# A convolution stage with three places for raw weights, three product buffers and later side transfers

## The chip, the cores and the metric

The kernel runs on one core of a Trainium2 chip. The metric is the device time of one execution in microseconds (us); the median over several executions is compared. One execution is also recorded by the hardware profiler, and all rows below are from that one.

## The reference, cut to what matters

A decoder trunk of two layers over 512 tokens with 1024 features. The change touches the first layer only, a convolution layer:

```python
def conformer_conv_branch(h, w_in, b_in, conv_w, conv_b, norm_g, norm_b, w_out, b_out):
    proj = h @ w_in + b_in                      # 512 x 1024 @ 1024 x 6144
    val, glu_gate, z = jnp.split(proj, 3, axis=-1)
    u = val * jax.nn.sigmoid(glu_gate)          # 2048 channels
    u = lax.conv_general_dilated(               # causal, 31 taps, one filter a channel
        u, conv_w[:, None, :], window_strides=(1,), padding=[(CONV_KERNEL - 1, 0)],
        dimension_numbers=('NWC', 'WIO', 'NWC'), feature_group_count=CONV_WIDTH) + conv_b
    u = jax.nn.silu(layer_norm(u, norm_g, norm_b))
    u = u * jax.nn.silu(z)
    return u @ w_out + b_out
```

Then comes `h = layer_norm(alpha * h + y, g, b)`, and an attention layer that the change does not touch. All is float32; a matrix product is made of three products of rounded parts (a high part and a low part of each operand, without low times low).

## The kernel before, in words

**Chunks.** The input projection of the first layer is cut into 48 chunks of 128 output channels, numbered c = 0 to 47. Chunks 2t and 2t + 1 (t = 0 to 15) are value and gate of channel tile t; chunks 32 + i (`Z0` + i) are z of tile i. Chunk c takes these steps, each engine in the order of its program:

- SP issues the load of 512 KB into a raw place `w_raw[c % 2]` (`load_columns`, L605), once chunk c - 2 has been split (`raw_free`), since there are two places.
- ACT rounds it into `w_hi[c % 4]` (`split_hi`, L1082), after the load has landed.
- POOL subtracts: `w_lo = w_raw - w_hi` (`split_lo`, L861).
- PE makes 24 matmuls (8 steps of 128 features, three products each, `columns`, L1961) into one of three PSUM banks.
- ACT keeps the bank (`keep_value` L1088, `keep_gate_half` L1094, `keep_z` L1228), POOL multiplies value and gate into `u` (`glu`, L873).

**Convolution beside it.** It is spread over all engines while PE makes the chunks:

- DVE makes twelve of the sixteen tiles (`convolve`, L1556), one tap an instruction, in two chains for each tile. ACT starts most chains (`start_chains`, L1136 and L1139). When DVE is done with its tiles it sums them (L1540, L1542) with a sum that POOL has made of others (`pool_csum`, L968), and PE multiplies the sum by ones for the mean, in the middle of chunk 43 (`sum_over_channels`, L2077). From there DVE, ACT and POOL make the variance.
- Tiles 1 and 7 (`GROUPED_TILES`): ACT multiplies four taps at a time (`BEFORE_GATING`), and POOL issues a DMA that adds the 1 MB to sums (`add_group`, L902). Before it issues one, POOL waits for the one before to have landed. The last taps of these tiles, and the first 22 of tile 4 (`LATE_TILE`), are single products: ACT writes one into `tap_product` (four buffers, `tap_times_u` L1176), and POOL adds it to `acc` one step later (`add_products`, L923). `AFTER_GATING`, `BEFORE_GATING[10]` and `IN_Z` say in which step which taps are made.
- Tiles 8 and 12 (`MATRIX_TILES`, m = 0 and 1) are made on PE as four packs each (`pack`, L2048 to L2051), after chunks 26 to 29 and 35 to 38. SP writes the tile's input to DRAM (`keep_u`, L611 and L613), reads it back shifted as stacks (`stack_u`, four DMAs for a pack, L622); ACT keeps each pack in one of two buffers (`keep_pack_after`, L1105), since all packs use one bank; SP moves its four parts (`move_parts`, L636) to free tiles.

**Order.** There is no planner: each engine's program is written out in one order. SP's order around the change is: the load of chunk c, then what `stack_after(c)` gives to that place, then the load of c + 1. ACT's order in step t (`value_gate`) is: w_hi of 2t, w_hi of 2t + 1, value of t - 1, packs kept, grouped taps, chain starts, gate of t - 1, products. POOL's is: w_lo of 2t and of 2t + 1, products of step t - 1 added, glu of t - 1, the group's DMA, and in steps 10 and 14 the low part of a matrix tile's input (L940), in step 15 the two matrices of the second matrix tile (L934).

Of the kernel before, what the change touches and what calls it, by code (L numbers as in the profile page):

```python
# [32 lines left out]
P = 128  # L33
# [53 lines left out]
RAW_SLOTS = 2  # L87
SLOTS = 4
# [34 lines left out]
def trunk_kernel(nc, x, positions, ln_g, ln_b, a_w_in, a_b_in, a_conv_w, a_conv_b, a_norm_g,  # L123
# [14 lines left out]
    with ExitStack() as ctx:  # L138
# [99 lines left out]
        tap_product = [at(f"tap_product{i}", reg_e, (2 + i) % 4 * TILE, [P, SEQ]) for i in range(4)]  # L238
# [84 lines left out]
        small_landed, table_landed = sem("small_landed"), sem("table_landed")  # L323
        w_landed = [sem(f"w_landed{i}") for i in range(RAW_SLOTS)]
# [203 lines left out]
        def landed_value(c):  # L528

            extra = 16 if isinstance(c, int) and c >= ROPE_CHUNK and (c - ROPE_CHUNK) % RAW_SLOTS == 0 else 0  # L530
            return 16 * (c // RAW_SLOTS + 1) + extra
# [66 lines left out]
        def _(sp):  # L598
            def raw_free(c):

                wait(sp, w_hi_ready, c - RAW_SLOTS + 1)
                wait(sp, w_lo_ready, c - RAW_SLOTS + 1)
# [48 lines left out]
            for r in range(RT):  # L651
                sp.dma_start(x_in[:, r, :], x_rows[:, r, :]).then_inc(x_landed[r], 16)
                if r % 2 == 1:
                    w = r // 2
                    load_columns(w, w_in_a, w * CONV_WIDTH)
# [7 lines left out]
            for c in range(2, Z0):  # L663
                raw_free(c)
                load_columns(c % 2, w_in_a, c % 2 * CONV_WIDTH + c // 2 * P)
                stack_after(c)
            for i in range(CT):
                raw_free(Z0 + i)
                load_columns(i % 2, w_in_a, 2 * CONV_WIDTH + i * P)
                stack_after(Z0 + i)  # L670
# [169 lines left out]
        def _(pool):  # L840
# [35 lines left out]
            def value_gate(t):  # L876
                for w in range(2):
                    if t == w == 0:
                        first_lo()
                    else:  # L880
                        split_lo(2 * t + w, w, (2 * t + w) % SLOTS)
                if t == GROUP_PAIRS[FIRST_GROUPS]:
                    sum_group(0)
                if t == GROUP_PAIRS[FIRST_GROUPS] + 1:
                    add_products(BEFORE_GATING[10])
                add_products(AFTER_GATING.get(t - 1, ()))
                if t > 0:
                    glu(t - 1, (t - 1) % 2)
                if t in GROUP_PAIRS:
                    add_group(GROUP_PAIRS.index(t))  # L890
                if t in BEGINS:
                    conv_input_lo(BEGINS.index(t))
                for m, low, at in ((0, 0, 4), (0, 1, 5), (1, 0, 15), (1, 1, 15)):
                    if t == at:
                        pack_matrices(m, low)
# [18 lines left out]
            def add_products(taps):  # L914

                for t, k in taps:
# [6 lines left out]
                    nc.gpsimd.tensor_tensor(acc[:, t, :], acc[:, t, :], tap_product[added_up_to((t, k)) % 4][:], ALU.add  # L923
# [47 lines left out]
            for i in range(CT):  # L971
                if 2 * (i - POOL_SUM_BEGINS) + 2 >= len(POOL_SUM) - 1:
                    sum_tiles(2 * (i - POOL_SUM_BEGINS))
                if i != 1:
                    split_lo(Z0 + i, i % 2, i % SLOTS)
                if i == 0:
                    split_lo(Z0 + 1, 1, 1)
# [100 lines left out]
        def _(act):  # L1078
            def split_hi(c, raw, slot, landed):
                act.wait_ge(w_landed[raw], landed)  # L1080
                wait(act, w_used, c - SLOTS + 1)
# [26 lines left out]
            def value_gate(t):  # L1108
                split_hi(2 * t, 0, 2 * t % SLOTS, 16 * (t + 1))
                keep_pack_after(2 * t - 3)  # L1110
                split_hi(2 * t + 1, 1, (2 * t + 1) % SLOTS, 16 * (t + 1))
# [38 lines left out]
            def tap_times_u(t, k):  # L1150
# [37 lines left out]
            for q in range(2 * RT):  # L1188
# [5 lines left out]
                if q == 3:  # L1194
                    act.wait_ge(w_landed[0], 16)
# [4 lines left out]
            split_hi(1, 1, 1, 16)  # L1200
            for w in range(2):
                split_hi(2 + w, w, 2 + w, 32)
# [29 lines left out]
            def z_split(i):  # L1232
                c = Z0 + i
                split_hi(c, c % 2, c % SLOTS, landed_value(c))
# [1125 lines left out]
```

## Time and profile before

| | |
|---|---|
| median of 3 executions | 800.81 us (800.72 to 802.31) |
| the profiled execution | 802.11 us, of which 800.3 us span from the first to the last instruction |
| PE / DVE / POOL / ACT busy | 98% / 72% / 65% / 51% of the span |
| convolution stage with input projection | about 0 to 296 us of the span |

The page of the profile gives each engine's busy time in the span. PE's matmuls are pipelined, so their busy time overlaps and says little; what tells lost time is the distance between the starts of two matmuls that follow each other, with the cause that the timeline gives in brackets. The chain of waits starts at the end and shows what was released by what.

### The profile page before, as it was taken

What the parts mean: (1) busy time and instruction counts of PE and PEld (TensorE: products, weight loads), DVE (VectorE), ACT (ScalarE), POOL (GpSimd) and SP (SyncE); (2) the same over time, 40 slices, a digit from 0 to 9 for tenths busy, and PEclk for the clock granted to TensorE, in tenths of its full rate; (3) what the DMA queues carried; (4) which work ended last, traced back from release to release, by engine and by line L of the source; (5) the groups of instructions that cost most, each with busy time, mean ns of one, the idle gap of its engine ahead of it and who ended that gap; (6) DMA issues with size and microseconds to landing.
All of it is one profiled execution on the core that took longest, in us unless ns stands there. A gap on an engine that the chain in (4) does not pass through costs nothing.

```text
span 800.3 us, 11082 instructions
## 1 busy us (share of the span) xinstructions
PE 782.1 (98%) x3779; PEld 660.6 (83%) x3779; DVE 578.8 (72%) x998; ACT 411.0 (51%) x717; POOL 521.6 (65%) x323
## 2 busy tenths in 40 slices
PE   8999999989899999999999999999999999999996
PEld 7888888878688878888888888889888988888885
DVE  2699999989999679975633390059777878876217
ACT  4465777673654577521333453157666676655110
POOL 4558988887998863872554457247777777377430
PEclk9999999999999999999999999999999999999999
DMA  6338885999843325632333225236567764663412
GB/s 226 106 106 205 182 192 160 229 215 212 193 139 103 116 79 160 210 114 71 106 107 113 86 79 170 66 104 177 178 188 217 190 202 134 198 191 120 157 53 105
DMA packets 129278, 119.12 MB, mean 149 GB/s; under 512 B 16618, under 2 KB 108880, under 8 KB 127820
## 3 DMA queue, kind: packets, MB, share of 16 engines
q1 hardware_dynamic: 127644, 106.95, 45.7%
q0 software_dynamic: 1584, 11.54, 7.7%
q8 instruction: 27, 0.44, 0.2%
q14 instruction: 23, 0.19, 0.1%
HBM read 86.68 MB, written 13.69 MB: 125 GB/s over the span
## 4 chain that ended last, share of the span: by engine, by line
PE 73%; POOL 9%; issue 6%; DMA 5%; SPq 3%; DVE 2%; ACT 2%; DVEq 0%; POOLq 0%; ACTq 0%
PE bank L1961 69%; POOL w_lo L861 5%; DMA w_raw<-in_a_w_in_dram 2%; POOL acc L923 2%; DMA prob_kept<-prob 2%; DMA x_in<-in_x_dram 1%; DVE acc L1639 1%; PE bank L2273 1%; POOL u L873 1%; PE bank L2274 1%; SPq L785 1%; SPq L622 1%; PE bank L2048 0%; DVE bank L1646 0%; PE bank L2051 0%
## 5 line engine op out<-in xcount | busy, mean ns | idle before, releaser
L861 POOL TENSOR_TENSOR w_lo<-w_raw,w_hi 128x1024 fp32r<-128x1024 f32 x102 | 254.0, 2510 | 135.8 <-ACT w_hi L1082 128.5
L1556 DVE SCALAR_TENSOR_TENSOR bank<-u,conv_w,bank 128x512 f32<-128x512 f32 x286 | 190.4, 748 | 2.4 <-ACT bank L1136 2.4
L1082 ACT ACTIVATE w_hi<-w_raw 128x1024 fp32r<-128x1024 f32 x102 | 107.0, 1056 | 111.9 <-DMA w_raw<-in_a_w_in_dram 46.1
L1961 PE MATMUL bank<-xt_hi,w_lo 128*128 128x512 f32 (+1 forms) x392 | 152.5, 389 | 2.9 <-ACT w_hi L1082 1.8
L1961 PE MATMUL bank<-xt_lo,w_hi 128*128 128x512 f32 (+1 forms) x392 | 151.1, 385 | 0.0
L1961 PE MATMUL bank<-xt_hi,w_hi 128*128 128x512 f32 (+1 forms) x392 | 150.9, 385 | 0.0
L1961 PEld LDWEIGHTS bank<-xt_hi,w_lo 128*128 128x128 f32 x392 | 73.8, 188 | 18.8 <-ACT w_hi L1082 2.2
L1961 PEld LDWEIGHTS bank<-xt_lo,w_hi 128*128 128x128 f32 x392 | 73.8, 188 | 15.1 <-issue 0.5
L1961 PEld LDWEIGHTS bank<-xt_hi,w_hi 128*128 128x128 f32 x392 | 73.8, 188 | 14.8
L1961 PE MATMUL bank<-ht_hi,w_lo 128*128 128x512 f32 (+1 forms) x208 | 76.0, 365 | 1.1 <-POOL w_lo L861 1.1
L1961 PE MATMUL bank<-ht_lo,w_hi 128*128 128x512 f32 (+1 forms) x208 | 75.8, 365 | 0.0
L1961 PE MATMUL bank<-ht_hi,w_hi 128*128 128x512 f32 (+1 forms) x208 | 75.8, 365 | 0.0
L1041 POOL TENSOR_TENSOR pt_lo<-prob_moved,pt_hi 128x512 fp32r<-128x512 f32 (+1 forms) x64 | 58.4, 945 | 17.7 <-ACT pt_hi L1426 17.7
L1010 POOL TENSOR_TENSOR bundle_lo<-bundle_raw,bundle_hi 128x1024 fp32r<-128x1024 f32 (+1 forms) x16 | 48.3, 3018 | 24.2 <-ACT bundle_hi L1353 24.2
L1961 PE MATMUL bank<-w_hi,fg_lo 128*128 128x512 f32 x128 | 50.1, 392 | 0.6 <-issue 0.6
L1961 PE MATMUL bank<-w_hi,g_lo 128*128 128x512 f32 x128 | 50.1, 392 | 0.2 <-DVE g_lo L1685 0.2
L1961 PE MATMUL bank<-w_hi,g_hi 128*128 128x512 f32 x128 | 49.8, 389 | 0.0
L1961 PE MATMUL bank<-w_hi,fg_hi 128*128 128x512 f32 x128 | 49.8, 389 | 0.0
L1961 PE MATMUL bank<-w_lo,g_hi 128*128 128x512 f32 x128 | 49.8, 389 | 0.0
L1961 PE MATMUL bank<-w_lo,fg_hi 128*128 128x512 f32 x128 | 49.8, 389 | 0.0
L1733 DVE SCALAR_TENSOR_TENSOR bank<-res,bank 128x512 f32<-128x512 f32 x16 | 11.0, 689 | 51.8 <-PE bank L1961 51.8
L1961 PEld LDWEIGHTS bank<-ht_hi,w_lo 128*128 128x128 f32 x208 | 39.2, 189 | 7.5 <-DVE ht_lo L1767 1.3
(239 smaller groups left out, 1746.5 us busy)
## 6 DMA issues: line engine op xcount, KB each, us to landing
w_raw<-in_a_w_in_dram SPq DMA_DIRECT2D x48, 512.0 KB, 4.1
w_raw<-in_b_w_in_dram SPq DMA_DIRECT2D x20, 512.0 KB, 3.7
prob_kept<-prob SPq DMA_DIRECT2D x16, 640.0 KB, 3.2
prob_moved<-prob_kept SPq DMA_DIRECT2D x64, 160.0 KB, 3.3
w_raw<-in_a_w_out_dram SPq DMA_DIRECT2D x16, 512.0 KB, 4.1
w_raw<-in_b_w_out_dram SPq DMA_DIRECT2D x16, 512.0 KB, 3.6
stacked<-u_kept SPq DMA_DIRECT2D x32, 132.0 KB, 5.8
bundle_raw<-in_b_w_uq_dram SPq DMA_DIRECT2D x16, 256.0 KB, 4.6
```

The lines of the kernel that those rows point to most:

```text
L622: sp.dma_start(stacked[PACK * j:PACK * (j + 1), :, g, :].bitcast(F32), u_kept[m][:, PACK * g:PACK * (g + 1), columns].rearrange("h c x -> ...
L785: sp.dma_start(prob_moved[QUAD * m:QUAD * (m + 1), :].rearrange("j (p n) -> j p n", p=QUADS), kept[:, m]).then_inc(prob_landed, 16)
L861: nc.gpsimd.tensor_tensor(w_lo[slot][:], w_raw[raw][:], w_hi[slot][:].bitcast(F32), ALU.subtract).then_inc(w_lo_ready, 1)
L873: nc.gpsimd.tensor_tensor(u[:, bass.ds(t, 1), PAD:].rearrange("p o n -> p (o n)"), val[slot][:], sig[slot][:], ALU.mult).then_inc(u_ready, 1)
L923: nc.gpsimd.tensor_tensor(acc[:, t, :], acc[:, t, :], tap_product[added_up_to((t, k)) % 4][:], ALU.add).then_inc(product_added, 1)
L1010: nc.gpsimd.tensor_tensor(bundle_lo[slot][part][:], bundle_raw[:, lo:hi], bundle_hi[slot][part][:].bitcast(F32), ALU.subtract).then_inc(bu ...
L1041: nc.gpsimd.tensor_tensor(turned_block(pt_lo, b), moved_block(b), turned_block(pt_hi, b).bitcast(F32), ALU.subtract).then_inc(pt_lo_ready, 1)
L1082: nc.scalar.activation(w_hi[slot][:], w_raw[raw][:], ACT.Copy).then_inc(w_hi_ready, 1)
L1556: nc.vector.scalar_tensor_tensor(out=inner[:] if k < TAPS - 1 else acc[:, t, :], in0=u[:, t, k:k + SEQ], scalar=conv_w[:, column:column + ...
L1639: nc.vector.scalar_tensor_tensor(out=acc[:, t, :], in0=bank[7][:], scalar=-1.0 / CONV_WIDTH, in1=acc[:, t, :], op0=ALU.mult, op1=ALU.add). ...
L1733: nc.vector.scalar_tensor_tensor(out=total[:], in0=rows_half, scalar=scale, in1=total[:], op0=ALU.mult, op1=ALU.add).then_inc(y_step, 1)
L1961: last = nc.tensor.matmul(out_ap, a, b, start=(start and n == 0 and m == 0), stop=(stop and n == len(parts) - 1 and m == 2))
```

## The change

- A third raw place `w_raw2` lies where `tap_product` 0 and 1 lay (the upper half of region `reg_e`). Chunks 0 to 41 use the three places in turn (`load_ring`, `split_ring`, one semaphore a place), so that the load of c waits for chunk c - 3 to be split. From chunk 42 on, two places are used as before, under the same waits.
- Four product buffers become three up to the last tap of tile 4: two `tap_product` and the unused row of `acc` of tile 7. After that, two. A product waits for the one three (two) before it to be added.
- The 20 taps of tile 4 in the steps up to 15 are spread otherwise: 3, 3, 3, 3, 3, 3, 2 in steps 6, 7, 8, 12, 13, 14, 15, before 3, 2, 2, 3, 3, 4, 2, 1 in steps 6, 7, 8, 9, 12, 13, 14, 15. Step 9 has none.
- On SP, `keep_u` comes after load 24 (32 for m = 1) and not 23 (31); `stack_u` after loads 26 to 29 (34 to 37) and not 25 to 28 (33 to 36); `move_parts` of m = 0 after loads 31 to 34 and not 30 to 33. Those of m = 1 stay after 39 to 42.

The diff, cut:

```diff
+RING = 3
+RING_END = 42
...
+        w_raw.append(at("w_raw2", reg_e, 2 * TILE, [P, CHUNK]))
...
-        tap_product = [at(f"tap_product{i}", reg_e, (2 + i) % 4 * TILE, [P, SEQ]) for i in range(4)]
+        tap_product = [at(f"tap_product{i}", reg_e, i * TILE, [P, SEQ]) for i in range(2)]
...
-        for t, n in ((6, 3), (7, 2), (8, 2), (9, 3), (12, 3), (13, 4), (14, 2), (15, 1)):
+        for t, n in ((6, 3), (7, 3), (8, 3), (12, 3), (13, 3), (14, 3), (15, 2)):
...
+        PLACES = 3
+        IN_RING = added_up_to((LATE_TILE, LATE_TAPS - 1))
+
+        def product_place(n):
+
+            if n <= IN_RING:
+                return (tap_product[0], tap_product[1], acc[:, LATER, :])[n % PLACES]
+            return tap_product[n % 2]
...
             def raw_free(c):
 
-                wait(sp, w_hi_ready, c - RAW_SLOTS + 1)
-                wait(sp, w_lo_ready, c - RAW_SLOTS + 1)
+                slots = RING if isinstance(c, int) and c < RING_END else RAW_SLOTS
+                wait(sp, w_hi_ready, c - slots + 1)
+                wait(sp, w_lo_ready, c - slots + 1)
+
+            def load_ring(c, source, column):
+                sp.dma_start(w_raw[c % RING][:].rearrange("p (k m) -> p k m", m=P),
+                             source[:, :, bass.ds(column, P)]).then_inc(ring_landed[c % RING], 16)
...
                 for m, begin in enumerate(BEGINS):
                     n = c - 2 * begin
-                    if n == 3:
+                    if n == 4:
                         keep_u(m)
-                    elif 5 <= n < 5 + PACKS:
-                        stack_u(m, n - 5)
+                    elif 6 <= n < 6 + PACKS:
+                        stack_u(m, n - 6)
                 for m, first in enumerate(PACKS_AT):
-                    if 0 <= c - first - 4 < PACKS:
-                        move_parts(m, c - first - 4)
+                    g = c - first - (5, 4)[m]
+                    if 0 <= g < PACKS:
+                        move_parts(m, g)
...
+                if t == LATER:
+                    pool.wait_ge(product_added, IN_RING)
...
-                    wait(act, product_added, max(0, n - 4))
-                    out = tap_product[n % 4][:]
+                    wait(act, product_added, max(0, n - (PLACES if n <= IN_RING else 2)))
+                    out = product_place(n)[:]
```

## Rows read from the trace of the kernel before

**Rows 1.** The page: each engine's busy us, share and instructions
```profile
PE 782.1 (98%) x3779; PEld 660.6 (83%) x3779; DVE 578.8 (72%) x998; ACT 411.0 (51%) x717; POOL 521.6 (65%) x323
```
**Rows 2.** Chain of waits, from 175 us: start, us, what
```profile
179.03 5.45 PE bank L1961 x24
```
**Rows 3.** Timeline of PE: start, us, instruction, [idle before, what ended it]
```profile
166.40 0.39 PE L1961 MATMUL bank<-xt_hi,w_hi 128*128 128x512 f32 x1
168.94 0.70 PE L2048 MATMUL bank<-stacked,matrix_lo 128*128 128x512 f32 x1 [2.15 <-ACT part_out L1105]
...
172.43 0.40 PE L1961 MATMUL bank<-xt_hi,w_hi 128*128 128x512 f32 x1
...
201.82 0.39 PE L1961 MATMUL bank<-xt_hi,w_hi 128*128 128x512 f32 x1
203.31 0.47 PE L1961 MATMUL bank<-xt_hi,w_lo 128*128 128x512 f32 x1 [1.10 <-issue]
...
208.61 0.39 PE L1961 MATMUL bank<-xt_hi,w_hi 128*128 128x512 f32 x1
210.83 0.47 PE L1961 MATMUL bank<-xt_hi,w_lo 128*128 128x512 f32 x1 [1.83 <-ACT w_hi L1082]
```
**Rows 4.** Table by stage: stretch, length, busy us (x) by engine, PEclk, DMA share, GB/s
```profile
120.00:135.00 15.00, 15.00 (x68) 12.43 (x67) 14.97 (x23) 12.05 (x18) 11.92 (x9) 1.00 0.47 145
...
165.00:175.00 10.00, 7.85 (x28) 5.97 (x28) 7.59 (x12) 8.32 (x14) 8.55 (x6) 0.83 1.05 240
```
**Rows 5.** Timeline of ACT around the first gap of PE
```profile
166.68 1.06 ACT L1082 ACTIVATE w_hi<-w_raw 128x1024 fp32r<-128x1024 f32 x1 [2.36 <-DMA w_raw<-in_a_w_in_dram]
```
**Rows 6.** Timeline of SP's queue: start, us of issuing, transfer
```profile
153.64 4.81 SPq L622 DMA_DIRECT2D stacked<-u_kept  x4
158.55 0.60 SPq L605 DMA_DIRECT2D w_raw<-in_a_w_in_dram  x1
...
188.84 0.53 SPq L605 DMA_DIRECT2D w_raw<-in_a_w_in_dram  x1
```
**Rows 7.** Loads of raw weights (L605), 140 to 204 us: us to landing
```profile
DMA to landing us min/median/max: 4.9/7.2/10.8
```
**Rows 8.** Group transfers of POOL (L902), 135 to 215 us: us to landing
```profile
DMA to landing us min/median/max: 7.0/9.1/10.7
```
**Rows 9.** Timeline of ACT before the second and third gap of PE
```profile
199.69 1.06 ACT L1082 ACTIVATE w_hi<-w_raw 128x1024 fp32r<-128x1024 f32 x1 [7.58 <-DMA w_raw<-in_a_w_in_dram]
```
**Rows 10.** Timeline of POOL: start, us, instruction, [idle before, what ended it]
```profile
150.42 2.70 POOL L861 TENSOR_TENSOR w_lo<-w_raw,w_hi 128x1024 fp32r<-128x1024 f32 x1
154.82 2.42 POOL L861 TENSOR_TENSOR w_lo<-w_raw,w_hi 128x1024 fp32r<-128x1024 f32 x1 [1.70 <-ACT w_hi L1082]
157.19 4.17 POOL L923 TENSOR_TENSOR acc<-acc,tap_product 128x512 f32<-128x512 f32 x3
...
164.41 2.39 POOL L861 TENSOR_TENSOR w_lo<-w_raw,w_hi 128x1024 fp32r<-128x1024 f32 x1 [0.99 <-ACT w_hi L1082]
...
167.81 2.37 POOL L861 TENSOR_TENSOR w_lo<-w_raw,w_hi 128x1024 fp32r<-128x1024 f32 x1 [1.01 <-ACT w_hi L1082]
...
192.29 2.68 POOL L861 TENSOR_TENSOR w_lo<-w_raw,w_hi 128x1024 fp32r<-128x1024 f32 x1
200.83 2.38 POOL L861 TENSOR_TENSOR w_lo<-w_raw,w_hi 128x1024 fp32r<-128x1024 f32 x1 [5.87 <-ACT w_hi L1082]
...
208.37 4.80 POOL L861 TENSOR_TENSOR w_lo<-w_raw,w_hi 128x1024 fp32r<-128x1024 f32 x2
```
**Rows 11.** Timeline of DVE: its one idle time in the taps, and its end
```profile
171.94 1.42 DVE L1556 SCALAR_TENSOR_TENSOR bank<-u,conv_w,bank 128x512 f32<-128x512 f32 x2 [2.38 <-ACT bank L1136]
...
263.17 0.70 DVE L1542 TENSOR_TENSOR bank<-bank,acc 128x512 f32<-128x512 f32 x1
267.67 0.69 DVE L1542 TENSOR_TENSOR csum<-bank,pool_csum 128x512 f32<-128x512 f32 x1 [3.80 <-POOL pool_csum L968]
```
**Rows 12.** Timeline of PE at the mean
```profile
269.58 1.02 PE L2077 MATMUL bank<-csum,ones 128*128 128x512 f32 x2
```

More of the change, by code:

```diff
@@ L323, in trunk_kernel @@
         small_landed, table_landed = sem("small_landed"), sem("table_landed")
+        ring_landed = [sem(f"ring_landed{i}") for i in range(RING)]
         w_landed = [sem(f"w_landed{i}") for i in range(RAW_SLOTS)]
@@ L530, in landed_value, with raw_of, ring_value @@
             extra = 16 if isinstance(c, int) and c >= ROPE_CHUNK and (c - ROPE_CHUNK) % RAW_SLOTS == 0 else 0
-            return 16 * (c // RAW_SLOTS + 1) + extra
+            return 16 * (c // RAW_SLOTS + 1 - RING_END // RAW_SLOTS) + extra
+        def raw_of(c):
+            return c % RING if isinstance(c, int) and c < RING_END else c % RAW_SLOTS
+        def ring_value(c):
+            return 16 * (c // RING + 1)
         POOL_SUM_BEGINS = 7
@@ L664, in _ @@
                 raw_free(c)
-                load_columns(c % 2, w_in_a, c % 2 * CONV_WIDTH + c // 2 * P)
+                load_ring(c, w_in_a, c % 2 * CONV_WIDTH + c // 2 * P)
                 stack_after(c)
@@ L668, in _ @@
                 raw_free(Z0 + i)
-                load_columns(i % 2, w_in_a, 2 * CONV_WIDTH + i * P)
+                if Z0 + i < RING_END:
+                    load_ring(Z0 + i, w_in_a, 2 * CONV_WIDTH + i * P)
+                else:
+                    load_columns(i % 2, w_in_a, 2 * CONV_WIDTH + i * P)
                 stack_after(Z0 + i)
@@ L880, in value_gate @@
                     else:
-                        split_lo(2 * t + w, w, (2 * t + w) % SLOTS)
+                        split_lo(2 * t + w, raw_of(2 * t + w), (2 * t + w) % SLOTS)
                 if t == GROUP_PAIRS[FIRST_GROUPS]:
@@ L922, in add_products @@
                     wait(pool, product_added, added_up_to((t, k)) - 1)
-                    nc.gpsimd.tensor_tensor(acc[:, t, :], acc[:, t, :], tap_product[added_up_to((t, k)) % 4][:], ALU.add
+                    nc.gpsimd.tensor_tensor(acc[:, t, :], acc[:, t, :], product_place(added_up_to((t, k)))[:], ALU.add
                                             ).then_inc(product_added, 1)
@@ L974, in _ @@
                 if i != 1:
-                    split_lo(Z0 + i, i % 2, i % SLOTS)
+                    split_lo(Z0 + i, raw_of(Z0 + i), i % SLOTS)
                 if i == 0:
-                    split_lo(Z0 + 1, 1, 1)
+                    split_lo(Z0 + 1, raw_of(Z0 + 1), 1)
                     add_products(AFTER_GATING[CT - 1])
@@ L1080, in split_hi, with split_ring, round_hi @@
                 act.wait_ge(w_landed[raw], landed)
+                round_hi(c, raw, slot)
+            def split_ring(c):
+                act.wait_ge(ring_landed[c % RING], ring_value(c))
+                round_hi(c, c % RING, c % SLOTS)
+            def round_hi(c, raw, slot):
                 wait(act, w_used, c - SLOTS + 1)
@@ L1108, in value_gate @@
             def value_gate(t):
-                split_hi(2 * t, 0, 2 * t % SLOTS, 16 * (t + 1))
+                split_ring(2 * t)
                 keep_pack_after(2 * t - 3)
-                split_hi(2 * t + 1, 1, (2 * t + 1) % SLOTS, 16 * (t + 1))
+                split_ring(2 * t + 1)
                 keep_value(t - 1, (t - 1) % ROUND)
@@ L1194, in _ @@
                 if q == 3:
-                    act.wait_ge(w_landed[0], 16)
+                    act.wait_ge(ring_landed[0], 16)
                     nc.scalar.activation(w_hi[0][:, 0:CHUNK // 2], w_raw[0][:, 0:CHUNK // 2], ACT.Copy
@@ L1199, in _ @@
                                          ).then_inc(w_hi_ready, 1)
-            split_hi(1, 1, 1, 16)
-            for w in range(2):
-                split_hi(2 + w, w, 2 + w, 32)
+            for c in range(1, SLOTS):
+                split_ring(c)
             act.wait_ge(vec_turned, 1)
@@ L1233, in z_split @@
                 c = Z0 + i
-                split_hi(c, c % 2, c % SLOTS, landed_value(c))
+                if c < RING_END:
+                    split_ring(c)
+                else:
+                    split_hi(c, c % 2, c % SLOTS, landed_value(c))
             def square(t):
```

2 lines of the change are left out of this document (1 added, 1 removed).

## The prediction

> **What bounds the kernel now.** I read the page first: PE is busy in 98% of the span [rows 1]. So the kernel ends when PE ends, and a change outside PE's own work can only give back PE's waits. Next the chain of waits, for the full pace: 24 matmuls of a chunk take 5.45 us, 0.227 us a matmul [rows 2]. Then the timeline of PE from 0 to 300 us, looking for two starts further apart than 0.227 us. Apart from x arriving at the start and a few tenths around the mean and variance, there are three places [rows 3]:
>
> - Gap 1, 166.40 to 168.94, before pack 1 (after chunk 27): 2.54 - 0.23 = 2.31 us. The eight matmuls from 168.94 to 172.43 then take 3.49 us and not 1.82, 1.67 us more; the table by stage has the granted clock at 0.83 for these ten microseconds, so part of them ran at the 1.2 GHz level [rows 4]. Together 3.98 us.
> - Gap 2, 201.82 to 203.31, before chunk 33: 1.49 - 0.23 = 1.26 us.
> - Gap 3, 208.61 to 210.83, before chunk 34: 2.22 - 0.23 = 1.99 us. No slow matmuls follow gaps 2 and 3.
>
> The sum is 7.2 us, 0.9% of the time, and all that this change can reach.
>
> **Where the gaps come from.** Gap 1: the second pack needs the bank that ACT keeps, and ACT stands before that at w_hi of chunk 29, for whose load it has idled 2.36 us; it starts at 166.68 [rows 5]. Load 29 was issued at 158.55 behind four stack transfers that held SP's queue for 4.81 us [rows 6]. Gaps 2 and 3: ACT idles 7.58 us for load 33 [rows 9], issued at 188.84 [rows 6]: 10.8 us to landing, the slowest of this stretch, where the median is 7.2 [rows 7]. The DMA engines' share is 1.05 at 165 to 175 us, and was 0.47 at 120 to 135 [rows 4]. POOL idles 5.87 us with ACT, and its w_lo of chunks 33 and 34 end at 203.21 and 210.7, where PE resumes [rows 10, 3].
>
> **Part by part.**
>
> *Third place.* The load of c goes out when chunk c - 3 is split, one chunk (5.45 us) ahead. Bytes, DMAs and instructions are the same. Load 29 then waits for w_lo of chunk 26, which ends at 150.42 + 2.70 = 153.1 [rows 10], and stands on SP ahead of the stacks of the last pack. It needs 7 to 11 us, lands by 164, and ACT comes to it at about 161. Cost: nothing before 42 chunks, same waits after.
>
> *Side transfers one load later.* Relative to the splits that release them they go out when they did before; loads have moved ahead of them. Passed on SP's queue: per pack four stack transfers, four moves, and for m = 1 both `keep_u`, whose wait for POOL's low part held load 32 and now holds load 33. By my sum of POOL below, that low part is there near 174, load 33 goes out behind four moves near 179, and lands at 186 to 190. ACT comes to it when chunk 30 is done, about 188. Then stacks and moves have four chunks more until pack 4. Nothing, as long as landings stay under about 11 us.
>
> *POOL, which is late next.* Its idle times in this stretch are 1.70 (chunk 27), 0.99, 1.01 and 5.87 us, all behind ACT's w_hi [rows 10]. Without the first, w_lo of 28 starts at 150.42 + 2.70 + 2.42 + 4.17 (three adds, 1.39 each) + 2.06 (glu and the group's issue: from the end of the adds at 161.36 to 163.42, where the idle 0.99 begins) = 161.8, not 164.4: 2.6 earlier. w_lo of 32 ends at 192.29 + 2.68 - 2.6 - 1.0 = 191.4. PE needs it at 192.6 (chunk 33's due start 202.05, less 5.45 and 3.98). w_lo of 34 starts at 208.37 - 2.6 - 1.0 - 5.9 + 1.4 = 200.3 and ends at 202.7; needed at 210.83 - 7.23 = 203.6. The 1.4 is the one add more that the new spread of taps puts before it (10, before 9). So POOL is in time by 1.2 and 0.9 us. That is thin.
>
> *Three product places.* ACT's product waits for the third before it to be added. With three products a step the last waits for the last add of the step before: POOL's third add, then 0.7 us of ACT, 1.06 of w_hi [rows 5], while POOL makes glu and issues the group (2.06). The two are about equal, so I take 0; bounds -0.4 (step 13 has three products for four, and step 10 needs no wait at all) and +0.7 us for each of the steps 12 to 15, in front of POOL's 0.9 us: 0 to 1.9 us for PE.
>
> *DVE, the second wall.* It works without a pause through its taps except 2.38 us at 169.6, for the chain that ACT starts late behind load 29 [rows 11]. Its own sums end at 263.17 + 0.70 = 263.87; then it idles 3.80 us for POOL's sum, which moves with PE's chunks. PE takes the mean at 269.58 without waiting [rows 12]. In the changed kernel the 2.38 go with load 29: sums at 261.5, csum 0.69 more, 262.2. POOL's sum was ready at 267.63 and comes 7.2 earlier, 260.4: in time. PE arrives at 269.58 - 7.23 = 262.35. DVE is just in time; I put 0.3 us for this meeting (bounds 0 and 2.4).
>
> *Sum.* 7.23 - 0.3 = 6.9 us. After the mean DVE, ACT, POOL and PE hang on each other as before and shift together. The profiled execution takes 802.11 us, 1.3 above the median of 800.81; 802.11 - 6.9 = 795.2 answers to 793.9 in the median.
>
> **A rule against it.** In the full stretch the group transfers on POOL's queue and the loads on SP's run together, loads landing after up to 10.8 us and groups after up to 10.7 [rows 7, 8]. The Trainium skill says (DMA: Bandwidth & Descriptors, Issuing engines are not separate DMA queues) that transfers of all issuing engines run on the same 16 DMA engines and interleave. By that rule alone an earlier load in a full stretch only changes places with a stack or a group, which is the third rival below.
>
> **Rivals.**
>
> 1. *Gap 1 goes, gaps 2 and 3 stay.* Load 33 still stands behind `keep_u` and four moves. If it takes 10.8 us to land and goes out 3 us later than I have it, ACT and POOL are late by what they are now. For: everything moves 4 us ahead, and so does the need. Against: one place more is 5.45 us. Gain 3.98: 796.8.
> 2. *DVE's wall.* Its 2.38 us do not go, or POOL's sum is late; PE waits at the mean for 2.4 us. Gain 4.8: 796.0. Against: ACT would start the chain at about 165.5, four microseconds ahead.
> 3. *Bandwidth.* The transfers are merely exchanged, waits move to stacks and groups, and the time stays: 800.8. Against: between 120 and 135 us the DMA engines are half idle [rows 4], so that one load more fits there.
> 4. *Slower: POOL held by its own groups.* Before it issues a group, POOL waits for the one before to land, and everything behind stands: glu, w_lo, matrices. There is one a step, and a step at PE's full pace is two chunks, 10.9 us; groups land after 9.1 in the median, 10.7 at most [rows 8]. From 10.9 on each microsecond of landing costs one for each of four steps (12 to 15). With 14 us: 4 x 3.1 = 12.4, less 0.9 of slack, against 7.2 given back: 4.3 slower, 805.1. The turn is at landings of about 12.9 us, since 4 x 2.0 = 8.0, about 7.2 + 0.9. The earlier loads push in that direction, the same bytes in the same time speak against it.
>
> **How the numbers follow.** Forecast 0.62, 793.9. Rival 1: 0.15. Rival 2: 0.11. Rival 3: 0.06. Rival 4: 0.06. The lower end is everything given back with 0.4 us of ACT's waits and a few tenths of scatter: 792.9. The upper end takes in rivals 1 and 2 with a microsecond, 797.8; what is left out is rivals 3 and 4 and some of the scatter, under 0.2. A difference under 0.2% (1.6 us) could not be told from no change. Faster: forecast and rivals 1 and 2, 0.87 with a little taken for weaker forms of them: 0.86. Same 0.08, slower 0.06.
>
> **What the changed profile would show.** No distance over 0.3 us between PE's starts from 20 to 260 us, and a granted clock of 1.00 at 165 to 175. Load 29 issued near 153, w_lo of 34 ending by 203.6, no idle DVE near 169. PE reaching the mean at about 262.4, DVE's last sum close to it, idle of DVE before POOL's sum under 1 us. Wrong: a wait of PE on w_lo or w_hi at chunks 32 to 34, groups landing after more than 11 us, or PE waiting for csum.

## The result, and the profile after

| | before | after |
|---|---|---|
| median, 12 executions each | 802.48 us (800.56 to 806.07) | 797.21 us (795.56 to 800.13) |
| ratio after / before | | 0.994, 95% interval 0.9926 to 0.9955 |
| the profiled execution (span) | 802.11 (800.3) us | 796.20 (794.4) us |
| PE: first matmul of chunk 0, matmul of the mean | 11.44, 269.58 us | 11.25, 263.42 us |
| the distance between these two | 258.14 us | 252.17 us |

The last row is the yardstick of all that follows. x lands at a slightly different time in each execution, so a span mixes that in; from chunk 0's first matmul to the mean's PE only works or waits for what the change can reach. There the changed kernel is 5.97 us shorter, where the prediction's sum has 6.9.

The page's busy times say nothing of it: they stay within 4 us of [rows 1] on every engine.

```profile
PE 779.9 (98%) x3779; PEld 659.5 (83%) x3779; DVE 581.1 (73%) x998; ACT 410.5 (52%) x717; POOL 522.2 (66%) x323
```

The timeline of PE, after, answers to [rows 3] and [rows 12]. Between 20 and 260 us one distance is left:

```profile
203.06 0.39 PE L2002 MATMUL bank<-xt_hi,w_hi 128*128 128x512 f32 x1
204.66 0.47 PE L2002 MATMUL bank<-xt_hi,w_lo 128*128 128x512 f32 x1 [1.21 <-issue]
...
263.42 0.59 PE L2118 MATMUL bank<-csum,ones 128*128 128x512 f32 x1
```

203.06 to 204.66 is 1.60, less 0.23 for a matmul: 1.37 us lost, in front of chunk 34. Gap 1 and gap 2 are gone, gap 3 has kept 1.37 of its 1.99. In the table by stage, after, the two stretches of [rows 4] show the granted clock at 1.00 in both, and a DMA share of 0.68 where it was 0.47, 1.10 where it was 1.05 (columns: stretch, length, PE, PEld, DVE, ACT, POOL, clock, DMA share, GB/s):

```profile
120.00:135.00 15.00, 15.00 (x68) 12.43 (x67) 14.96 (x24) 12.41 (x18) 10.30 (x7) 1.00 0.68 178
...
165.00:175.00 10.00, 10.00 (x46) 8.22 (x45) 9.97 (x16) 8.98 (x15) 9.48 (x8) 1.00 1.10 247
```

The timeline of ACT, after, has w_hi of chunk 29 and then, 35 us on, the wait that remains ([rows 5, 9] of before):

```profile
162.47 1.06 ACT L1121 ACTIVATE w_hi<-w_raw 128x1024 fp32r<-128x1024 f32 x1 [2.14 <-DMA w_raw<-in_a_w_in_dram]
164.01 0.59 ACT L1144 ACTIVATE part_out<-bank 128x512 f32<-128x512 f32 x1
...
198.07 0.69 ACT L1186 ACTIVATE bank<-acc,vec 128x512 f32<-128x512 f32 x1 [4.77 <-DMA acc<-part_out]
199.92 1.99 ACT L1121 ACTIVATE w_hi<-w_raw 128x1024 fp32r<-128x1024 f32 x2
```

The wait for load 29 is nearly as long as before, 2.14 for 2.36 us, but it ends 4.2 us earlier (166.68 less 162.47), so that the pack is kept (164.01) before PE wants its bank. The wait of 4.77 us is not for a load: L1186 is `start_parts(0)`, ACT's start of the sums of the first matrix tile, and it waits for the last of the moved parts. SP's queue and POOL's, after, around it ([rows 6, 10] of before):

```profile
185.59 2.69 SPq L662 DMA_DIRECT2D u<-part_out  x3
188.33 0.60 SPq L662 DMA_DIRECT2D acc<-part_out  x1
```
```profile
188.48 5.01 POOL L891 TENSOR_TENSOR w_lo<-w_raw,w_hi 128x1024 fp32r<-128x1024 f32 x2
...
199.48 1.30 POOL L955 TENSOR_TENSOR acc<-acc 128x512 f32<-128x512 f32 x1 [2.06 <-ACT acc L1215]
...
202.18 4.75 POOL L891 TENSOR_TENSOR w_lo<-w_raw,w_hi 128x1024 fp32r<-128x1024 f32 x2
```

The last move goes out at 188.33 and lands at 198.0, 9.7 us later. The kernel before has this wait too, which the prediction doesn't mention: 2.17 us, for a move that went out at 197.60 and landed in 5.8 us. The timeline of ACT, before:

```profile
203.50 0.69 ACT L1147 ACTIVATE bank<-acc,vec 128x512 f32<-128x512 f32 x1 [2.17 <-DMA acc<-part_out]
```

There the load of chunk 33 had held ACT first [rows 9]. After, behind ACT's wait stand its product, on which POOL waits 2.06 us, and w_hi of chunk 34. The two w_lo at 188.48 are those of chunks 32 and 33, in time. Those of 34 and 35 start at 202.18 (the row joins the two); the first ends at 204.56, and at 204.66 PE goes on.

Groups of POOL (L932, 135 to 215 us) and loads of raw weights (L627, 140 to 204 us), after, against [rows 8, 7]:

```profile
DMA to landing us min/median/max: 8.0/11.0/12.6
...
DMA to landing us min/median/max: 6.7/7.9/10.2
```

The groups land 2 us later than before, the median load 0.7 us later, the slowest load 0.6 earlier.

### The profile page after: what moved, and what is told of

Read it like the earlier page. It is cut to its first block, busy times and chain, and to the rows that moved or that the text cites. A ratio compares the mean times of both kernels' runs of the same rounds, so it can differ in the third digit from the quotient of the medians.

```text
span 794.4 us, 11082 instructions
## 1 busy us (share of the span) xinstructions
PE 779.9 (98%) x3779; PEld 659.5 (83%) x3779; DVE 581.1 (73%) x998; ACT 410.5 (52%) x717; POOL 522.2 (66%) x323
## 4 chain that ended last, share of the span: by engine, by line
PE 93%; DVE 2%; DMA 1%; issue 1%; POOL 1%; ACT 0%; SPq 0%; DVEq 0%; ACTq 0%
PE bank L2002 88%; PE bank L2314 1%; PE bank L2315 1%; DMA x_in<-in_x_dram 1%; POOL pt_lo L1073 1%; DVE acc L1680 1%; DMA prob_moved<-prob_kept 0%; DVE bank L1687 0%; PE bank L2092 0%; PE bank L2089 0%; PE bank L2090 0%; PE bank L2187 0%; PE bank L2307 0%; POOL w_lo L891 0%; PE bank L2305 0%
```

## The experiments

Times are medians against the kernel before on the same chip; "stretch" is the distance from chunk 0's first matmul to the mean's in the profiled execution (before 258.14, after 252.17). Where it says "one execution" there is no interval. The first four cut the change into its parts.

| kernel | stretch, us | ratio (95%) | median, us |
|---|---|---|---|
| e1: third place, side transfers in the old order | 250.94 | 0.9923 (0.9897 to 0.9949) | 796.58 |
| e2: two places, side transfers one load later | 257.17 | 1.0021 (1.0001 to 1.0042) | 803.38 |
| e3: two places, old order: only products and spread | 253.83 | 0.9965 (0.9945 to 0.9986) | 799.77 |
| e4: after, the matrix tile's sums started a step later | 251.08 | 0.9915 (0.9886 to 0.9943) | 795.47 |
| e6: e4 with three more copies on DVE | 253.23 | one execution | 798.71 |
| e7: before with the new spread of taps | 253.38 | 0.9945 (0.9925 to 0.9964) | 797.72 |
| e8: e1 with e4's later start | 250.98 | 0.9933 (0.9913 to 0.9952) | 796.89 |
| e9: after, side transfers two loads later | 258.70 | 1.0026 (1.001 to 1.0042) | 803.53 |
| e10: after with 8 transfers more | 254.75 | one execution | 800.79 |
| e11: e7, load 33 held behind POOL's group | 259.04 | 1.0014 (0.9994 to 1.0033) | 803.91 |
| e12: before, one add moved by a step | 254.39 | 0.9966 (0.9948 to 0.9984) | 799.51 |
| e13: e8 with one tap taken from DVE | 251.02 | 0.9921 (0.9899 to 0.9943) | 795.67 |

### e1: the third place, and the old order of side transfers

```diff
-                    if n == 4:
+                    if n == 3:
                         keep_u(m)
-                    elif 6 <= n < 6 + PACKS:
-                        stack_u(m, n - 6)
+                    elif 5 <= n < 5 + PACKS:
+                        stack_u(m, n - 5)
...
-                    g = c - first - (5, 4)[m]
+                    g = c - first - 4
```

> The changed kernel with the side transfers back in their old order: keep_u after load 23 (31), stacks after 25 to 28 (33 to 36), the moves of m = 0 after 30 to 33. Three places, three product buffers and the new spread of taps stay. Theory 'the third place does it': the first gap is gone, loads 28 and 29 land by 163, and the gain is that of the whole change, 5 to 6 us against the kernel before. Rival 'the order does it': SP stands after load 30 at the first pack to be kept and after load 31 at the low part of the second matrix tile's input (about 174 us), so that load 32 goes out near 178 and load 33 near 185, at the earliest 3 us later than needed by ACT at 188: PE gets a gap of 1 to 3 us before chunk 33 or 34 and the gain is 3 to 4 us.

Measured: no gap of PE is left up to 260 us, in front of chunk 34 neither, and the stretch is 1.2 us shorter than with the later side transfers. Load 32 went out at 182.12 and load 33 at 185.30, behind `keep_u` as the rival had it, but they landed in time (load 33 in 5.9 us). In this execution chunk 0's first matmul starts at 14.25 us and not near 11, so all its times stand 3 us late. The two ratios' intervals overlap; it is the gap that tells the two kernels apart. The part that I had costed at nothing costs something, and the old order of transfers was not in the way of the third place.

### e2: side transfers one load later with two places

```diff
-RING = 3
+RING = 2
```

> The changed kernel with two raw places in turn and not three; side transfers one load later, product buffers and spread of taps as changed. If the third place does it: load 33 waits for chunk 31 to be split and the third gap stays, gap 1 shrinks by the 2 to 5 us that load 29 no longer stands behind four stacks; gain 0 to 3 us. If the order does it: gain 4 us or more.

Against e3, below, which differs in the order on SP alone, the stretch is 257.17 - 253.83 = 3.3 us longer. Of these, 1.0 us lies in front of pack 1, where e2 loses 2.71 us and e3 1.75 (load 29 landed 0.9 us later, counted from chunk 0's first matmul); the rest lies further on. ACT at the start of the matrix tile's sums and PE at chunk 34, in e2:

```profile
203.09 0.69 ACT L1186 ACTIVATE bank<-acc,vec 128x512 f32<-128x512 f32 x1 [5.71 <-DMA acc<-part_out]
```
```profile
209.66 0.47 PE L2002 MATMUL bank<-xt_hi,w_lo 128*128 128x512 f32 x1 [2.13 <-issue]
```

It is the same wait as in the changed kernel, 5.71 for 4.77 us, with PE's gap at the same place: 209.66 less 207.14 and 0.23, 2.29 us lost for 1.37. In e3 that gap does not exist, so 2.3 of the 3.3 us are this wait's.

### e3: the product places and the spread alone

```diff
-RING = 3
+RING = 2
```

and on SP the edit of e1.

> Two raw places and side transfers in their old order; only three product buffers and the new spread of taps are left of the change. My sum took 0 for them: the three gaps of PE at 166, 202 and 209 us stay with 7.2 us in all (within 1 us), the time within 1.5 us of the kernel before. If the buffers cost what I put as their bound, the sum of the gaps grows by up to 1.9 us.

This was the surprise. With neither the third place nor the later transfers the stretch is 4.3 us shorter than before. PE has a gap at 167.53 (1.75 us lost) and one at 176.22 (1.22), both in front of a pack; gaps 2 and 3 do not exist. So the third place is worth 253.83 - 250.94 = 2.9 us (e3 to e1), and most of the rest comes from the part that I had costed at 0.

### e4: the sums of the first matrix tile started one step later

```diff
-        PARTS_START_IN_Z = {1: 0, 12: 1}
+        PARTS_START_IN_Z = {2: 0, 12: 1}
```

> The changed kernel, but ACT starts the sum of the first matrix tile's parts in step i = 2 of z, behind w_hi of chunk 34, and not in step i = 1. Theory: the gap of 1.37 us that is left before chunk 34 comes from ACT standing 4.77 us at that start for the last move to land, with two products and w_hi of 34 behind it and POOL's w_lo of 34 behind these. Then the gap goes, w_lo of 34 ends by 203, PE is at the mean about 262.1 and waits there 0.2 to 0.5 us for csum (ready at 262.4 before); gain 1 us more than the change. Rival 'POOL is too slow there by itself, or the load is late': w_lo of 34 still ends after 204 and the gap stays above 1 us.

ACT, in e4, at the same instruction:

```profile
197.38 0.69 ACT L1186 ACTIVATE bank<-acc,vec 128x512 f32<-128x512 f32 x1 [0.47 <-DMA acc<-part_out]
```

0.47 us for 4.77, PE's gap before chunk 34 is gone and the stretch 1.1 us shorter (what is left is 0.4 us at 172.59). The transfers and their order are the same, and the last move lands as late as there (186.5 us after chunk 0's first matmul, 186.8 in the changed kernel). Only the reader has gone, and the gap with it: that this wait makes the gap is shown. The same wait is 2.81 us in e1, 2.94 in e3 and 2.46 in e7, and PE has no gap in front of chunk 34 there: in these kernels a wait of up to 2.9 us costs PE nothing, and 4.77 does.

### e7 and e12: where the spread's gain comes from

e7 is the kernel before with one line changed; e12 moves a single add from step 13 to step 14:

```diff
-        for t, n in ((6, 3), (7, 2), (8, 2), (9, 3), (12, 3), (13, 4), (14, 2), (15, 1)):
+        for t, n in ((6, 3), (7, 3), (8, 3), (12, 3), (13, 3), (14, 3), (15, 2)):
```
```diff
-        for t, n in ((6, 3), (7, 2), (8, 2), (9, 3), (12, 3), (13, 4), (14, 2), (15, 1)):
+        for t, n in ((6, 3), (7, 2), (8, 2), (9, 3), (12, 3), (13, 3), (14, 3), (15, 1)):
```

> The kernel before with nothing changed but the spread of tile 4's taps (3, 3, 3, 3, 3, 3, 2 in steps 6, 7, 8, 12, 13, 14, 15; none in step 9). Two places, four product buffers, old order. The kernel with products and spread alone gained 2.8 us, where I had taken 0. Theory: the gain is the spread's, since step 10 no longer makes three adds on POOL and ACT no longer waits there, and everything after it starts earlier: then this gains 2 to 4 us as well, and the gaps at 202 and 209 us are gone or under 1 us together. Rival: it comes from the buffers: then the gaps stay near 3.2 us and the time is within 1 us of the kernel before.

> The kernel before with one tap alone moved: 3, 2, 2, 3, 3, 3, 3, 1 products in steps 6, 7, 8, 9, 12, 13, 14, 15 (step 13 had four, step 14 two). Step 9 keeps its three, so POOL and ACT are as busy as before in step 10. If the gain of the new spread comes from POOL's add less before the low parts of chunks 30 and 31 (load 32 and 33 go out 1.4 us or more earlier, 33 ahead of the group), this gains 3 us, and load 33 lands in 5 to 6 us. If it comes from step 10, the load still stands behind the group, the gaps at 202 and 209 us stay near 3.2 us, and the time is that of the kernel before within 1 us.

e7 takes 4.8 of the whole change's 6.0 us, e12 takes 3.75: about gaps 2 and 3 (1.26 + 1.99 = 3.25), which are gone in both. The rest lies at the packs: gap 1 and its slow matmuls took 3.98 us before; e7 loses 1.29 and 1.25 us in front of packs 1 and 2, e12 2.34 and 1.22. (e7 against e3, four product places against three: 253.38 and 253.83, with overlapping intervals; the two profiled stretches put three places at 0.45 us.) Load 33 on SP's queue and the group of step 15 on POOL's, first in the kernel before, then in e7, then in e12; the first row of each pair is the load but in the kernel before, where the group is ahead:

```profile
187.77 0.86 POOL L902 DMA_DIRECT2D second_sums<-z_a  x1
```
```profile
184.82 0.53 SPq L605 DMA_DIRECT2D w_raw<-in_a_w_in_dram  x1
...
186.44 0.86 POOL L902 DMA_DIRECT2D second_sums<-z_a  x1
```
```profile
185.76 0.53 SPq L605 DMA_DIRECT2D w_raw<-in_a_w_in_dram  x1
...
187.35 0.88 POOL L902 DMA_DIRECT2D second_sums<-z_a  x1
```

Before, load 33 went out at 188.84 [rows 6], 1.1 us behind the group. And the landings of load 33: before, e7, e12.

```profile
DMA to landing us min/median/max: 10.8/10.8/10.8
```
```profile
DMA to landing us min/median/max: 5.0/5.0/5.0
```
```profile
DMA to landing us min/median/max: 4.7/4.7/4.7
```

One add of 1.39 us fewer before POOL's w_lo of chunks 30 and 31 sends the load out 3.1 us (e12) and 4.0 us (e7) earlier, or 2.7 and 3.7 counted from chunk 0's first matmul, ahead of the 1 MB. That is more than the add: in e12 load 32 goes out 1.8 us earlier, and the four moves between it and load 33 hold SP's queue 1.2 us less (185.00 to 188.74 before, 183.15 to 185.67 in e12). Load 33 then lands 9 to 10 us earlier, and gaps 2 and 3 with their 7.58 us of ACT [rows 9] are gone.

### e11: load 33 held behind the group

e7, with one wait more on SP: load 33 waits for POOL's second matrix high part, which POOL makes behind its group.

```diff
+                if i == 1:
+                    sp.wait_ge(matrix_hi_ready, 2)
```

> The kernel before with the new spread of taps, where load 33 goes out at 184.8 us, ahead of POOL's last but one megabyte of group sums (186.4), and lands after 5.0 us. Here SP also waits, ahead of load 33, for the high matrix of the second matrix tile, which POOL makes right behind that group's issue: load 33 goes out near 189.3. Theory 'who is first': the load now shares the DMA engines with the group and takes 9 to 11 us, lands near 199, w_lo of 33 ends near 203 where PE needs it at 200.3: a gap of 2 to 3 us before chunk 33, as in the kernel before. Rival 'only the later start counts': it still takes 5 to 6 us, lands by 195, w_lo of 33 ends by 198.5 and PE has no gap there.

The stretch went from 253.38 to 259.04. But the loss is not where I looked for it. SP's queue, ACT, POOL, PE and the table by stage of e11:

```profile
189.58 0.39 SPq L605 DMA_DIRECT2D w_raw<-in_a_w_in_dram  x1
...
196.80 0.53 SPq L605 DMA_DIRECT2D w_raw<-in_a_w_in_dram  x1
```
```profile
196.89 1.06 ACT L1084 ACTIVATE w_hi<-w_raw 128x1024 fp32r<-128x1024 f32 x1 [6.31 <-DMA w_raw<-in_a_w_in_dram]
...
202.49 1.04 ACT L1084 ACTIVATE w_hi<-w_raw 128x1024 fp32r<-128x1024 f32 x1
```
```profile
198.03 2.40 POOL L863 TENSOR_TENSOR w_lo<-w_raw,w_hi 128x1024 fp32r<-128x1024 f32 x1 [4.24 <-ACT w_hi L1084]
...
207.02 2.34 POOL L863 TENSOR_TENSOR w_lo<-w_raw,w_hi 128x1024 fp32r<-128x1024 f32 x1
```
```profile
209.46 0.54 PE L1963 MATMUL bank<-xt_hi,w_lo 128*128 128x512 f32 x1 [3.21 <-issue]
```
```profile
205.00:215.00 10.00, 6.79 (x23) 5.18 (x22) 9.90 (x16) 6.05 (x8) 9.70 (x7) 0.83 0.71 181
```

Load 33 went out at 189.58 and landed in 7.3 us, neither 5 nor 10.8, just in time for PE's chunk 33. Load 34 stood on the same queue behind it, four stacks and four moves (196.80), but it landed at 202.3, and ACT took it at 202.49 without a wait. What was late is POOL: it idled 4.24 us for w_hi of 33, and between the end of w_lo of 33 (200.44) and the start of w_lo of 34 (207.02) its order has 6.6 us of adds and glu, where the kernel before has 5.2, one add less. w_lo of 34 ended at 209.36. PE lost 3.37 us in front of chunk 34, and its next matmuls were slow (mean granted clock 0.83 from 205 to 215 us). So it is shown that holding load 33 back by 5 us takes all the spread's gain away: it comes back as gap 3 of the kernel before, by ACT's wait and what POOL has to do behind it. That the group in front makes a load twice as slow is seen in the kernel before (10.8) and not in this strength here (7.3): of the landing's share and of the issue's, this run settles only that the issue alone is enough.

### e8: does the later start help by itself?

e1's edit and e4's together.

> Three places, old order of the side transfers, and the start of the first parts' sum in step 2 of z. If the left gap came from the last move landing late, there is none in the old order and this adds nothing to three places alone: from the first chunk's matmul to the mean 250.9 us, as there (251.0) and with the changed order and the later start (251.1); gain 6 to 7 us. If each of the two helps by itself, it is under 250.5 us.

250.98, where e1 has 250.94: no difference. The later start repairs the later moves, and where they are not late it is worth nothing. PE has no gap left in this kernel, and meets DVE:

```profile
261.47 0.39 PE L2002 MATMUL bank<-xt_hi,w_hi 128*128 128x512 f32 x1
262.00 1.10 PE L2118 MATMUL bank<-csum,ones 128*128 128x512 f32 x2
```
```profile
261.16 0.69 DVE L1583 TENSOR_TENSOR csum<-bank,pool_csum 128x512 f32<-128x512 f32 x1
```

0.53 between PE's starts, less 0.23: 0.3 us of wait for the sum of DVE.

### e9: side transfers two loads later

```diff
-                    if n == 4:
+                    if n == 5:
                         keep_u(m)
-                    elif 6 <= n < 6 + PACKS:
-                        stack_u(m, n - 6)
+                    elif 7 <= n < 7 + PACKS:
+                        stack_u(m, n - 7)
...
-                    g = c - first - (5, 4)[m]
+                    g = c - first - (6, 4)[m]
```

> The changed kernel with the side transfers two loads later instead of one. Theory: the last move of the first matrix tile then goes out behind load 35, which waits for w_lo of chunk 32 (191 us), so it is issued near 195 and lands near 204 instead of 198; ACT starts the parts 6 us later, and the gap before chunk 34 grows from 1.4 to 6 to 8 us. The time is at or above that of the kernel before (0 to 2 us more). Rival, lateness costs nothing by itself: the gap stays below 2 us.

The size was as expected, 6.5 us more than after, but the place was not: the larger part lies at the last pack. ACT, PE and POOL of e9:

```profile
182.78 0.60 ACT L1144 ACTIVATE part_out<-bank 128x512 f32<-128x512 f32 x1 [6.78 <-DMA acc<-part_out]
...
204.12 0.69 ACT L1186 ACTIVATE bank<-acc,vec 128x512 f32<-128x512 f32 x1 [4.83 <-DMA acc<-part_out]
```
```profile
183.53 0.77 PE L2089 MATMUL bank<-stacked,matrix_lo 128*128 128x512 f32 x1 [3.80 <-ACT part_out L1144]
```
```profile
173.21 0.88 POOL L932 DMA_DIRECT2D second_sums<-acc  x1 [2.27 <-DMA second_sums<-z_a]
```

There are two `part_out` buffers. A kept pack waits until the pack two before it has been moved out, 6.78 us here, and PE waits 3.80 for the bank. Then comes the start of the sums once more (4.83), with 1.43 us lost on PE. And POOL waits 2.27 us for a group that took 13.0 us to land: the seed of the fourth rival.

### e10: more traffic

Eight transfers of 256 KB from DRAM to DRAM, read by nobody, one behind each of the loads 24 to 31:

```diff
+                if 24 <= c < 32:
+                    sp.dma_start(spare[c - 24], x_rows[:, 0, 0:BANK]).then_inc(spare_kept, 16)
```

> The changed kernel with eight transfers more, of 256 KB each from DRAM to DRAM, one behind each load from 24 to 31 (dead work). It tests my fourth rival: groups land in the changed kernel after 11.0, 11.2 and 12.6 us. Theory: with 2 MB more in that stretch they land after 13 us and more, POOL stands before the issue of the next group with everything behind it, and PE gets gaps of 5 us or more in all between 160 and 215 us; the time is 3 to 8 us above the changed kernel's. Rival: the loads' lateness alone counts, POOL waits for no group.

Groups (L937), POOL and ACT of e10:

```profile
DMA to landing us min/median/max: 8.1/11.0/12.6
```
```profile
160.58 0.88 POOL L937 DMA_DIRECT2D second_sums<-z_a  x1 [1.19 <-DMA second_sums<-acc]
```
```profile
198.57 0.69 ACT L1191 ACTIVATE bank<-acc,vec 128x512 f32<-128x512 f32 x1 [5.75 <-DMA acc<-part_out]
```

The groups did not go past the 12.6 us that the changed kernel has already; POOL waited 1.19 us and PE lost nothing there. The 2.6 us came from the moved part once more: 5.75 for 4.77 at L1191, and 2.33 us lost before chunk 34 for 1.37, which is 1.0 us; the other 1.6 are eight slow matmuls behind it. Counted from chunk 0's first matmul the last move went out 2.0 us later than in the changed kernel, and it landed in 8.7 us for 9.7. In this one execution the added bytes thus delayed the side transfers on SP's queue first, and not the groups.

### e6 and e13: DVE's wall

e6 is e4 with three copies more on DVE ahead of its sum, with which nothing is computed; e13 is e8 with one tap of tile 4 given from DVE to ACT and POOL.

```diff
+                for n in range(3):
+                    wait(dve, extra_done, n)
+                    nc.vector.tensor_copy(bank[SUM_BANK][:], acc[:, 0, :]).then_inc(extra_done, 1)
+                dve.wait_ge(extra_done, 3)
```
```diff
-        LATE_TILE, LATE_TAPS = 4, 22
+        LATE_TILE, LATE_TAPS = 4, 23
...
-        for t, n in ((6, 3), (7, 3), (8, 3), (12, 3), (13, 3), (14, 3), (15, 2)):
+        for t, n in ((6, 3), (7, 3), (8, 3), (9, 1), (12, 3), (13, 3), (14, 3), (15, 2)):
```

> The changed kernel with the later start of the parts' sum, and three copies more on DVE before its own sums (dead work, about 0.7 us each, 2.1 us in all). Theory 'DVE is the second wall': csum was ready 1.0 us before PE took it, so PE now waits 1.1 us at the mean, and the time from first chunk to mean grows from 251.1 to 252.2 us. Rival: DVE has more slack than the trace says, PE does not wait.

> Three places, old order of the side transfers, later start of the parts' sum, and one tap of tile 4 less on DVE (ACT and POOL make it as a product in step 9, which had none). There PE had no gap left and waited 0.3 us for csum at the mean. Theory: DVE is the wall, its sums end 0.66 us earlier, PE does not wait: first chunk to mean 250.6 us, 0.3 to 0.4 less. Rival: POOL's one add more in step 10 makes w_lo of a later chunk late, and the stretch is longer than 251.0.

DVE and PE of e6 at the mean, then PE of e13 in front of pack 2:

```profile
263.52 0.69 DVE L1584 TENSOR_TENSOR csum<-bank,pool_csum 128x512 f32<-128x512 f32 x1
```
```profile
264.36 1.10 PE L2123 MATMUL bank<-csum,ones 128*128 128x512 f32 x2 [2.33 <-DVE csum L1584]
```
```profile
172.75 0.39 PE L2002 MATMUL bank<-xt_hi,w_hi 128*128 128x512 f32 x1
173.25 0.47 PE L2089 MATMUL bank<-stacked,matrix_lo 128*128 128x512 f32 x1
```

PE waits 2.33 us for DVE, twice what was expected; a part of the difference is one tap that took 1.78 us where it takes 0.85 in e4 (last section). The wall stands where the prediction has it: what DVE takes more, PE waits for. The other way nothing was gained: e13's stretch is 251.02 for e8's 250.98. The theory held at the mean, where csum is done 0.86 us earlier (counted from chunk 0's first matmul) and PE no longer waits. But PE now loses 0.27 us in front of pack 2 (173.25 less 172.75 and 0.23), where e8 loses nothing: ACT and POOL stand 0.7 us later from 150 us on (POOL's w_lo at 149.94 for 149.26), and ACT keeps the bank of pack 1 that much later. That fits the tap that they took over, and it takes back what DVE gave. The three kernels with the best ratios (e4 0.9915, e13 0.9921, e1 0.9923) can't be told apart, and their intervals overlap with that of the changed kernel.

## Why the prediction was right, and where it was not

The time was in the range and the direction right; the gain in the profiled stretch was 6.0 us for 6.9.

**What bounds.** Right: all of the gain is PE's gaps. 7.23 in three gaps before, 1.37 in one after, makes 5.86 of the 5.97 us.

**Gap 1 and its clock.** Right. Load 29 went out at 152.24 ("near 153"), ACT's w_hi of 29 came at 162.47 (expected about 161), the granted clock is 1.00. DVE's 2.38 us went with it. e3 to e1 prices the third place at 2.9 us. Of the 3.98 us, the 1.67 of slow matmuls were not bound to come with the gap: e12 loses 2.34 us at the same place at a granted clock of 1.00.

**POOL's schedule.** Right to some tenths up to chunk 33: load 33 out at 178.86 ("near 179"), landed at 186.24 ("186 to 190"), w_lo of 32 done at 191.14 (191.4). w_lo of 34 ended at 204.56 where I had 202.7, and where I had written that 203.6 is the last that PE can bear.

**The step that failed.** *Side transfers one load later*, which I closed with "Nothing, as long as landings stay under about 11 us". I had followed the loads behind the moves, and the stacks to their packs, and not the moves to their reader. The last move of m = 0 goes out one load later and takes 9.7 us, and ACT's `start_parts(0)` waits for it, with a product, POOL and w_hi of chunk 34 behind. The trace of before would have told it: ACT's idle times between 190 and 212 us hold 2.17 us for `part_out`, and I had read only those for loads. The later side transfers cost 3.3 us with two places (e2 against e3), 2.3 of them by this wait, and 1.2 us with three (after against e1); e4 shows the cause by moving the reader.

**Three product places.** The bounds were 0 to 1.9 and I took 0; e3 against e7 gives 0.45, not to be told from 0. That was right for the buffers. The *spread*, in the same part, I treated as one add more in front of w_lo of 34 (1.4 us). Not its size but its reach was missed: by e7 it would have given 4.8 us alone, since it lets load 33 go out ahead of a group of POOL. In the forecast gaps 2 and 3 went by the third place. Whether the third place with the old spread would have done that was not tried; so how the credit for gaps 2 and 3 is to be shared between the two is open, and with it whether that part of the forecast came true for its own reason or by luck. In the order spread, three products, third place, later transfers, the stretch moved by -4.8, +0.4, -2.9 and +1.2 us, together -6.0.

**DVE's wall.** Put at 0.3 us at the mean. In the changed kernel PE comes 1.1 us later than forecast (263.42 for 262.35) and does not wait; csum was done at 262.39 (262.2 forecast):

```profile
261.70 0.69 DVE L1583 TENSOR_TENSOR csum<-bank,pool_csum 128x512 f32<-128x512 f32 x1 [0.19 <-POOL pool_csum L1000]
```

In e1 and e8, where PE has no gap, it waits 0.3 us, as put. DVE's idle before that sum is 0.19 us, where it had 3.80 [rows 11].

**The rivals.** The chances of the forecast and rivals 1 and 2 add up to 0.88, not to 0.87. Rival 1 was right in its place and wrong in its cause: of gap 3 1.37 us stayed, but not by load 33. Rival 2, at 2.4 us, did not come; e6 calls it up. Rival 3 rested on a rule of the Trainium skill (DMA: Bandwidth & Descriptors, Issuing engines are not separate DMA queues): that transfers of all issuing engines interleave on the same 16 DMA engines. The trace agrees in the landings, with groups at 11.0 for 9.1 and moves at 5.1 to 9.8 for 2.3 to 5.8 us, but not in the time: the exchanged waits fell on transfers that had room, but for one, and the one is the 1.37 us. Rival 4 had groups turn at 12.9 us; they came to 12.6 (after, and e10) and 13.0 (e9), and POOL waited 0.5 in all, 1.19 and 2.27 us for them. The changed kernel is thus close to that edge. It did not decide.

**The median.** Forecast 793.9, measured 797.21. Of the 3.3 us 1.7 are the kernel before, which in these executions had 802.48 and not 800.81, and the rest is a gain of 5.3 us in the medians for 6.9.

## What to carry to other kernels

When transfers are moved on a queue, follow each to the instruction that reads it, with the landing time of the *busier* stretch, and not only those that stand behind it: one late reader on another engine cost 1.1 to 2.3 us here. Where engines take turns, an add of 1.4 us more or less on the engine next in line is no local price; look which transfers change their order by it. And a reader with slack can be moved behind its transfer before a buffer is added: e4 does it with one number.

## What the runs showed of the hardware

**The landings of one load.** The load of chunk 33, 512 KB, landed in 10.8 us when it was issued 1.1 us behind a 1 MB group (before), in 4.3 to 5.9 us when 0.7 to 2.5 us ahead of it (e1, e2, e3, e7, e8, e12, e13), in 7.3 us when 3.0 us behind it (e11), and in 6.4 to 7.4 us when 4.9 to 5.1 us ahead (e4, e6, e10, after). The 10.8 us stand in one trace alone.

**The clock after a gap.** Matmuls at the 1.2 GHz level (starts 0.43 us apart, not 0.23) followed losses of 2.31 (before), 2.33 (e10), 2.49 (e6), 3.37 (e11) and 3.96 us (e9), and did not follow 1.37 (after), 1.99 (before), 2.29 (e2), 2.34 (e12) and 2.71 us (e2, at 166.16). Between 2.3 and 2.7 us both happened. Where it came it made eight to twelve matmuls 0.2 us longer each, so these gaps cost 1.6 to 2.6 us more than they show.

**DVE held by POOL.** One tap of DVE that reads two operands in SBUF and one scalar (L1608, 128x512) takes 0.75 us (e10) to 2.32 us (e9), with the same work. POOL and DVE of the changed kernel, then of e4:

```profile
249.62 2.41 POOL L891 TENSOR_TENSOR w_lo<-w_raw,w_hi 128x1024 fp32r<-128x1024 f32 x1
```
```profile
250.63 1.96 DVE L1608 SCALAR_TENSOR_TENSOR bank<-u,conv_w,acc 128x512 f32<-128x512 f32 x1
```
```profile
248.14 2.41 POOL L891 TENSOR_TENSOR w_lo<-w_raw,w_hi 128x1024 fp32r<-128x1024 f32 x1
```
```profile
250.25 0.85 DVE L1608 SCALAR_TENSOR_TENSOR bank<-u,conv_w,acc 128x512 f32<-128x512 f32 x1
```

In both the tap ends 0.56 us after POOL's instruction beside it: 250.63 + 1.96 = 252.59 for 249.62 + 2.41 = 252.03, and 251.10 for 250.55 by the rounded rows. In all fourteen traces of this case the distance is 0.56 to 0.58 us. Begun early, the tap takes until POOL is done. POOL's next add is held in turn: in both kernels it starts before the tap has ended and takes 1.74 and 1.75 us, where the one behind it takes 1.29. That fits what the Trainium skill says (SBUF — State Buffer, SBUF: two separate sides): a DVE operation with two SBUF inputs and a GpSimd operation that reads SBUF share a port pair as an exclusive lock, held for the whole instruction. The traces agree with it in these numbers; no run here took POOL's instruction away.

**Scatter between executions.** Chunk 0's first matmul starts at 10.8 to 14.3 us in these traces, with the same transfers up to there, and from the mean's matmul to the end they take 530.8 to 533.5 us. In one profile a microsecond of span is thus no evidence; a gap in a named place is.
